# Weights times values of two attention heads, summed together at the end of a round

## The reference, cut to what matters

```python
q, k, v, fg = jnp.split(proj, [D_MODEL, 2 * D_MODEL, 3 * D_MODEL], axis=-1)
log_f = jax.nn.log_sigmoid((fg + b_f).astype(jnp.float32))
c = jnp.cumsum(log_f, axis=1).transpose(0, 2, 1)
...
logits = jnp.einsum("bhqd,bhkd->bhqk", q_i, k).astype(jnp.float32) * scale
logits = logits + c_i[..., None] - c[:, :, None, :]
mask = pos_k[None, :] <= pos_q[:, None]
logits = jnp.where(mask, logits, -jnp.inf)
probs = jax.nn.softmax(logits, axis=-1)
return jnp.einsum("bhqk,bhkd->bhqd", probs.astype(v.dtype), v)
```

## Time and profile before

| what | us |
|---|---|
| median of 3 runs | 1323.13 (1322.67 to 1324.28) |
| the profiled execution | 1323.11 |
| its span, first to last instruction | 1321.1 |
| PE busy | 1289.9 (98%) |
| PE weight loads busy | 1018.2 (77%) |
| DVE busy | 536.7 (41%) |
| ACT busy | 408.1 (31%) |
| POOL busy | 859.0 (65%) |
| granted clock of TensorE over the span | 0.993 of full |

### The profile page before, as it was taken

How to read it: one execution, slowest core, us unless ns; L and a number is a source line. 1 busy time by engine, 2 the same in 40 slices (tenths; PEclk the granted TensorE clock), 3 DMA queues, 4 the chain that set the end, 5 groups by cost and what they waited for, 6 DMA issues and landing times.

```text
span 1321.1 us, 17615 instructions
## 1 busy us (share of the span) xinstructions
PE 1289.9 (98%) x5758; PEld 1018.2 (77%) x5758; DVE 536.7 (41%) x826; ACT 408.1 (31%) x678; POOL 859.0 (65%) x1166
## 2 busy tenths in 40 slices
PE   6999999998999999999999999999999999999998
PEld 3766666676888888888888877877888888888886
DVE  6533344445444444411063357173444444301252
ACT  1443343411434333300033368112334333300041
POOL 6343445525978787777767645737877878777573
PEclk9999999998999999999999999998999999999999
DMA  5111113211232223333324222312322223333221
GB/s 184 52 48 64 48 48 112 80 49 64 96 106 96 100 95 127 95 112 96 96 86 168 81 81 64 112 48 84 108 95 96 98 99 128 111 104 96 80 89 56
DMA packets 57146, 120.58 MB, mean 91 GB/s; under 512 B 3744, under 2 KB 35808, under 8 KB 56592
## 3 DMA queue, kind: packets, MB, share of 16 engines
q1 hardware_dynamic: 56048, 117.45, 27.1%
q10 hardware_dynamic: 1056, 2.58, 0.6%
HBM read 117.83 MB, written 2.20 MB: 91 GB/s over the span
## 4 chain that ended last, share of the span: by engine, by line
PE 81%; issue 6%; ACT 3%; POOL 3%; DVE 2%; POOLq 2%; ACTq 1%; DMA 1%; DVEq 0%; SPq 0%
PE bank L408 17%; PE bank L410 16%; PE bank L409 16%; PE bank L428 6%; PE bank L427 6%; PE bank L429 6%; PE bank L521 3%; PE bank L659 2%; PE bank L664 2%; PE bank L660 2%; POOLq L391 2%; ACT probs L1236 1%; POOL w_lo L394 1%; POOL far_lo L394 1%; POOLq L389 1%
## 5 line engine op out<-in xcount | busy, mean ns | idle before, releaser
L394 POOL TENSOR_TENSOR w_lo<-stage,w_hi 128x256 fp32r<-128x256 f32 x800 | 589.5, 768 | 29.4 <-issue 0.3
L390 POOL TENSOR_SCALAR w_hi<-stage 128x1024 fp32r<-128x1024 f32 x200 | 211.9, 1060 | 175.2 <-PE bank L429 72.8
L408 PE MATMUL bank<-x_hi,w_hi 128*128 128x512 f32 x704 | 274.2, 390 | 0.0
L409 PE MATMUL bank<-x_lo,w_hi 128*128 128x512 f32 x704 | 273.9, 389 | 0.0
L410 PE MATMUL bank<-x_hi,w_lo 128*128 128x512 f32 x704 | 273.9, 389 | 0.0
L388 POOL TENSOR_TENSOR waiter<-waiter 128x1 f32<-128x1 f32 x112 | 24.4, 218 | 234.0 <-PE bank L410 159.9
L410 PEld LDWEIGHTS bank<-x_hi,w_lo 128*128 128x128 f32 x704 | 132.2, 188 | 27.4
L409 PEld LDWEIGHTS bank<-x_lo,w_hi 128*128 128x128 f32 x704 | 132.2, 188 | 27.4
L408 PEld LDWEIGHTS bank<-x_hi,w_hi 128*128 128x128 f32 x704 | 132.2, 188 | 27.2
L1038 DVE SCALAR_TENSOR_TENSOR tmp<-bank,cols,tmp 128x511 f32<-128x511 f32 x88 | 66.0, 750 | 209.7 <-ACT tmp L1292 198.7
L408 PE MATMUL bank<-in_hi,w_hi 128*128 128x512 f32 x320 | 137.7, 430 | 1.9 <-POOL w_lo L394 1.2
(11 more groups left out here) (166 smaller groups left out, 1758.6 us busy)
## 6 DMA issues: line engine op xcount, KB each, us to landing
stage<-w_square SPq DMA_DIRECT2D x164, 512.0 KB, 3.3
stage<-w_down SPq DMA_DIRECT2D x44, 512.0 KB, 3.7
rows<-norm_rows SPq DMA_DIRECT2D x4, 1024.0 KB, 5.7
outT<-x SPq DMA_DIRECT2D x8, 256.0 KB, 2.0
x<-xT SPq DMA_DIRECT2D x2, 512.0 KB, 5.0
x<-xT ACTq DMA_DIRECT2D x2, 512.0 KB, 8.3
p_in<-pT ACTq DMA_DIRECT2D x2, 512.0 KB, 3.3
w_ai<-w_lru SPq DMA_DIRECT2D x1, 1024.0 KB, 8.0
```

The lines of the kernel that those rows point to most:

```text
L390: pool.tensor_scalar(high[:, s, :], stage[:, s, :], 1.0, 0.0, ALU.mult, ALU.add)
L394: piece = pool.tensor_tensor(low[:, s, to], stage[:, s, to], high[:, s, to].bitcast(F32), ALU.subtract)
L408: pe.matmul(out, w_hi[:, s, c:c + P], m_hi, start=first, stop=False)
L409: pe.matmul(out, w_hi[:, s, c:c + P], m_lo, start=False, stop=False)
```

## The change

The sums leave the pieces of head 0. Head 1's pieces now hold the sums of both heads: for each key tile, head 0's matmul and then head 1's. `probs_t` gets a second half, one for each head, and pv_done is counted once a round in place of once a head. The positions of head 1's pieces are as before.

```diff
--- before.py
+++ after.py
@@ -43,7 +43,7 @@
 PIECES = 4
 
 TURN_AT = 2
-FIRST_AT = (1, 1, 4, 5, 6)
+FIRST_AT = (1, 1, 4)
 SECOND_AT = (0, 1, 3, 4, 5)
 GATES_AT = (1, 4)
 GATE_BANK = (4, 0, 5, 1)
@@ -207,7 +207,7 @@
         v_tok = place("v_tok", [P, QT, P], F32, a)
         tri = QT * (QT + 1) // 2 * P
         probs = place("probs", [P, 2, tri], F32, a)
-        probs_t = place("probs_t", [P, tri], F32, a)
+        probs_t = place("probs_t", [P, 2, tri], F32, a)
         z_chan = place("z_chan", [HEADS, SEQ], F32, a)
         fg = place("fg", [P, 6, QT * HEADS], F32, a)
         up_to = place("up_to", [P, SEQ], F32, a)
@@ -510,17 +510,18 @@
                                           probs[:, h, a0:a0 + P], ident[:])
                 mm.then_inc(pt_done, 1)
 
-            def sum_values(j, h, tiles):
-
-                if h == 0 and tiles[0] == 0:
-
+            def sum_values(j, tiles):
+
+
+                if tiles[0] == 0:
                     pe.wait_ge(vt_read, j + 1)
                 for kt in tiles:
                     w, c0 = (QT - kt) * P, sum(QT - t for t in range(kt)) * P
-                    pe.wait_ge(pt_read, j * 6 + (h * 3 + min(kt, 2) + 2))
-                    mm = pe.matmul(banks[7][h * HEAD_DIM:(h + 1) * HEAD_DIM, kt * P:SEQ],
-                                   v_tok[:, kt, h * HEAD_DIM:(h + 1) * HEAD_DIM], probs_t[:, c0:c0 + w],
-                                   start=(kt == 0), stop=(kt == QT - 1), skip_group_check=True)
+                    pe.wait_ge(pt_read, j * 6 + (3 + min(kt, 2) + 2))
+                    for h in range(2):
+                        mm = pe.matmul(banks[7][h * HEAD_DIM:(h + 1) * HEAD_DIM, kt * P:SEQ],
+                                       v_tok[:, kt, h * HEAD_DIM:(h + 1) * HEAD_DIM], probs_t[:, h, c0:c0 + w],
+                                       start=(kt == 0), stop=(kt == QT - 1), skip_group_check=True)
                 if tiles[-1] == QT - 1:
                     mm.then_inc(pv_done, 1)
 
@@ -534,9 +535,9 @@
 
             def head(j, h, at):
 
-                steps = (lambda: turn_probs(j, h, 0), lambda: turn_probs(j, h, 1),
-                         lambda: turn_probs(j, h, 2), lambda: sum_values(j, h, (0, 1)),
-                         lambda: sum_values(j, h, (2, 3)))
+                steps = [lambda: turn_probs(j, h, 0), lambda: turn_probs(j, h, 1), lambda: turn_probs(j, h, 2)]
+                if h == 1:
+                    steps += [lambda: sum_values(j, (0, 1)), lambda: sum_values(j, (2, 3))]
                 beside = {}
                 for k, step in zip(at, steps):
                     beside.setdefault(k, []).append(step)
@@ -1016,7 +1017,7 @@
                 normalise(j - 1, 1)
                 queries(j, True)
                 keys_low(j)
-                dve.wait_ge(pv_done, j * 2)
+                dve.wait_ge(pv_done, j)
                 mixed(j - 1)
             maxima(PAIRS - 1, 0)
             normalise(PAIRS - 1, 0)
@@ -1242,11 +1243,11 @@
                 for step, (bank, a0, w) in enumerate(((5, 0, 512), (6, 512, 384), (5, 896, 384))):
                     act.wait_ge(pt_done, j * 6 + (h * 3 + step + 1))
                     if step == 0 and weighed:
-                        act.wait_ge(pv_done, j * 2 + h)
-                    act.copy(probs_t[:, a0:a0 + w], banks[bank][:, 0:w]).then_inc(pt_read, 1)
+                        act.wait_ge(pv_done, j)
+                    act.copy(probs_t[:, h, a0:a0 + w], banks[bank][:, 0:w]).then_inc(pt_read, 1)
 
             def outputs(j):
-                act.wait_ge(pv_done, j * 2 + 2)
+                act.wait_ge(pv_done, j + 1)
                 act.copy(mix_hi[:, bass.ds(j, 1), :].rearrange("p a n -> p (a n)"), banks[7][:])\
                     .then_inc(mix_hi_ready, 1)
 
@@ -1257,7 +1258,7 @@
                 turned_probs(j, 0, not first)
                 if project_it:
                     keys(j_next, True)
-                turned_probs(j, 1, True)
+                turned_probs(j, 1, not first)
                 outputs(j)
                 if project_it:
                     values(j_next, True)
```

## The result

| kernel | median, us | lowest to highest | ratio to the kernel before, 95% interval |
|---|---|---|---|
| before | 1323.16 (4 runs) | 1322.67 to 1324.28 | 1 |
| changed | 1310.38 (4 runs) | 1309.04 to 1311.21 | 0.9899 [0.9887, 0.9911] |

The change makes the kernel faster by 12.8 us, 1.0%. It lies 0.3 us from the time of the third rival, full overlap (1310.1).

The account below looks back on a forecast made before the run. The prediction took PE's instruction stream plus its few waits to bound the kernel. With 13.85 us gone and 6.1 added, 7.7 less than 1323.11 gave 1315.4 us, range 1311.5 to 1327.0.

Parts of the forecast that it names:

- the third rival: Sums of both heads: full overlap, each head in its own queue, 0.8 us added, 1310.1 us; chance 0.07.
- the addition of 6.1 us: Head 0's passes between head 1's: overlap offset by one pass adds 0.76 us a round, 6.1 in all.
- no later stage gives anything back: After the attention stage: PE's own progress releases everything, so the 7.7 us gain is kept.
- Head 0's sums cost 2.85 us: Before the third projection, seven rounds: 1.25 us gained each, 8.75 in all; 1.60 becomes waiting for DVE's query read.
- Six waits for head 1's copies go: Head 1's third turning: PE's wait for ACT's copies goes, 0.39 us in six rounds, 2.35 us.
- The last round gains 2.75 us: Last round, with no queries to read: PE reaches head 1's first turning 2.75 us sooner.
- starts are in order: PE's queue at the sums: head 1's first pass can start only beside head 0's second, one pass of offset.
- the 13.85 gone: Attention stage: total time removed, 8.75 + 2.35 + 2.75 = 13.85 us, before the added streaming.
- each pass would wait: Sums of both heads: halves don't overlap, 17.1 us added, 1326.4 us, slower; first rival, chance 0.24.
- No change of shape is added: At head 1's existing places: head 0's passes fit in without further shape changes, so the added cost is streaming alone.
- The clock: Wait before the third projection: 1.60 us idle lowers TensorE's clock, 1.2 us lost in seven rounds, 1323.5 us; chance 0.03.

Follow-up runs that it names:

- the runs with blocks of eight and six passes: Changed kernel with a round's sums at one place: all head 0's eight passes first, 1319.81 us; six ahead of head 1's first, 1314.98 us.
- the run with one half: Changed kernel with head 1's sums sent to partitions 0 to 63, head 0's half, too: 1326.53 us, ratio 1.0021.
- the one-place kernel: Changed kernel with all eight sums of a round at one place of the third projection, still by turns: 1307.48 us, ratio 0.9869.
- the kernel with blocks of four: Changed kernel with head 0's two sums, then head 1's two, at each of the two places, not by turns: 1309.9 us, ratio 0.9895.

## Why the prediction was wrong

The direction, the sums that had to be counted and the new wait were right. One term of the sum, the addition of 6.1 us, was sized by a mechanism that the runs refute, and a smaller step, that no later stage gives anything back, did not hold in the profiled executions.

- **Head 0's sums cost 2.85 us, of which 1.25 are gained and 1.60 become a wait.** Right. Without the wait the third projection would have begun at 173.65 + 0.23 = 173.88; it began at 175.47, 1.59 later. The profile shows 1.42 us of it as idle time, since the modelled end of the last matmul reaches 0.17 us into it.
- **Six waits for head 1's copies go, 0.39 us each.** Right: from 178.89 to the turning at 179.13 it is 0.24 us, in place of 186.48 - 185.86 = 0.62 in the earlier trace rows.
- **The last round gains 2.75 us.** Right: from the sums of the round before it to its own it is 260.31 - 235.69 = 24.62 us, in place of 273.69 - 246.32 = 27.37.
- **The addition of 0.76 us a round.** This step failed. I wrote that "starts are in order", that head 1's first pass stands in the queue behind head 0's second and can only start beside it. The two first passes start 0.01 us apart. What is left of the addition is 0.05 us or less a round: 29.34 - 1.25 - 0.39 = 27.70, against 27.74 measured. For eight rounds that is 5.7 us less than I counted, and 1315.4 - 5.7 = 1309.7. The profiled executions say the same for the whole attention: at the first transpose behind it the lead is 13.36 us, so of the 13.85 gone only 0.5 came back, not 6.1. My reading was of a trace in which neighbouring passes always shared columns, and there they must follow each other; I took this for a rule of the queue. Full overlap was on my list with a chance of 0.07, as "each head in its own queue". Its time came out, but its mechanism does not hold as I wrote it: the runs with blocks of eight and six passes show that some order does bind, at a distance of four. The change, by turns, stays within it.
- **The Trainium skill's rule** ("TensorE: Matmul & The Clock Gate", section "Part 3: Packing small matmuls") that loads of weights overlap a matmul in flight only when the row group differs. The prediction made of it that each pass would wait, and that gives 1326.4, the time of the run with one half. The trace disagrees. Both heads use all 128 rows here, and the loads of the changed kernel at its first sums,

```profile
180.24 0.19 PEld L522 LDWEIGHTS bank<-probs_t,v_tok 128*64 128x64 f32 x3 [0.37 <-issue]
```

start at 180.24, 180.24 and, the third, at 180.30, when both first passes (180.25) are running. The sentence is about loads; that the passes would then wait too was my own step, and they overlap entirely.
- **No change of shape is added.** Right: 180.25 to 181.90 is 1.65 us, the same as for one head. What leaving a place and coming back costs, 0.35 us by my reading, the one-place kernel shows: 2.9 us in eight rounds.
- **The clock.** Right. Across the new wait and behind it the granted clock stayed at full speed, 2.4 GHz (start and end, length, PE busy, clock, DMA share, GB/s; kernel after):

```profile
173.90:175.50 1.60, 0.18 (x2) 1.00 0.02 5
175.50:179.00 3.50, 3.50 (x19) 1.00 0.00 0
```

- **"No later stage gives it back."** Not so in the two profiled executions. The first transpose behind the attention's output projection comes at 313.36 us before and at 300.00 after, a lead of 13.36 us; at the end it is 11.6. The wait for POOL's low parts is longer after the change, but the lead behind it is still 317.64 - 304.25 = 13.39 us. It goes in the matmuls that follow, which run at the low clock for longer (the tables of the last section): where the twelve matmuls with x_lo begin, it is 323.70 - 311.46 = 12.24. The second layer repeats it: 897.54 - 885.37 = 12.17 at the same matmul, and 11.65 (903.78 - 892.13) where those with x_lo begin. Before:

```profile
313.36 1.12 PE L436 MATMUL bank<-ident,x 128*128 128x128 f32 x4 [2.91 <-DVE x L880]
...
317.64 0.80 PE L659 MATMUL bank<-x_hi,w_hi 128*128 128x512 f32 x1 [0.42 <-POOL w_lo L394]
...
323.70 2.88 PE L664 MATMUL bank<-x_lo,w_hi 128*128 128x512 f32 x12
...
897.54 0.80 PE L659 MATMUL bank<-x_hi,w_hi 128*128 128x512 f32 x1 [0.42 <-POOL w_lo L394]
```

and after:

```profile
300.00 0.66 PE L436 MATMUL bank<-ident,x 128*128 128x128 f32 x4 [2.91 <-DVE x L881]
...
304.25 0.80 PE L660 MATMUL bank<-x_hi,w_hi 128*128 128x512 f32 x1 [1.30 <-POOL w_lo L394]
...
311.46 2.88 PE L665 MATMUL bank<-x_lo,w_hi 128*128 128x512 f32 x12
...
885.37 0.79 PE L660 MATMUL bank<-x_hi,w_hi 128*128 128x512 f32 x1 [0.85 <-POOL w_lo L394]
```

The change need not be the cause. From that transpose to the matmuls with x_lo it is 10.34 us before and 11.46 after, but 10.29 in the kernel with blocks of four, which holds the change too (its wait for POOL is 0.42 us), and from 10.23 to 12.30 in the other kernels. What decides in an execution when the clock falls and comes back is not shown. It is of the size of the changed kernel's spread of 2.2 us; whether it is behind that is open.

## What to carry to other kernels

Before moving work away from a place, ask which wait it had covered: here 1.6 of 2.85 us went into a wait for another engine, and reordering that engine's two steps, worth nothing before, then gained 8.8 us. When a cost can't be seen in the trace, the forecast should not rest on an order that was only seen where the operands forced it.

## What the runs showed of the hardware that was not expected

- Head 1's first pass starts 0.01 us after head 0's when it stands two passes behind it in the program, and 0.02 us after when it stands four behind. At six and eight it was late by 0.91 and 1.56 us: it came with the pass four places ahead of it.
- Around and behind the 2.91 us of waiting in front of the transposes the clock fell to 1.2 GHz, half of full speed, for some microseconds, and where that began and ended differed between the two kernels (start and end, length, PE busy, clock, DMA share, GB/s). Before, then after:

```profile
313.30:316.30 3.00, 2.27 (x7) 0.50 0.58 175
316.30:319.30 3.00, 2.58 (x7) 0.50 0.12 38
319.30:322.30 3.00, 3.00 (x15) 0.94 0.38 142
```

```profile
299.90:302.90 3.00, 2.23 (x8) 0.83 0.52 175
302.90:305.90 3.00, 1.70 (x5) 0.50 0.19 48
305.90:308.90 3.00, 3.00 (x10) 0.53 0.36 132
```

Before, the matmuls are slow from the first transpose on, and fast again at 319.5, 6.2 us later. After, they are slow from about 301.9 to 308.5: about as long but later, so that dense matmuls behind POOL's wait fall into it. The waits of 1.42 to 1.54 us in the rounds never had this effect: from 57 to 284 us of the changed kernel the granted clock is 1.00.
